# A decoder layer on one core: attention in two steps for a head pair, banks and small sums rearranged

## The reference, cut to what matters

```python
h = modulate(rms_norm(x, g_ffn1), sh1, sc1)
x = x + 0.5 * (1 + gt1) * swiglu(h, w1, w3, w2)
h = modulate(rms_norm(x, g_mix), sh2, sc2)
cq, ckv, kidx, widx, mq, mk, mv, ga, gb = split_cols(h @ w_in)
y_dsa  = dsa_attention(...) @ w_proj_dsa     # 8 heads, top-128 keys by an index score
y_moba = moba_attention(mq, mk, mv) @ w_proj_moba   # 8 heads, causal
y = sigmoid(ga) * y_dsa + sigmoid(gb) * y_moba
x = x + (1 + gt2) * (y @ w_out)
h = modulate(rms_norm(x, g_ffn2), sh3, sc3)
x = x + 0.5 * (1 + gt3) * swiglu(h, w1b, w3b, w2b)
out = rms_norm(x, g_final)
```

## Time and profile before

| | us |
|---|---|
| median of 3 runs | 1148.05 (1146.92 to 1148.19) |
| profiled execution, own time | 1148.91 |
| its span | 1147.0 |
| PE busy | 1121.8 |
| VectorE busy | 564.9 |
| ScalarE busy | 502.2 |
| mean granted PE clock | 0.997 |

### The profile page before, as it was taken

One profiled execution on the slowest core, in us unless ns is written; L12 is line 12 of the kernel. 1 busy time (PEld: TensorE's weight loads), 2 busy tenths in 40 slices (PEclk: granted clock), 3 DMA queues, 4 the chain that ended last, 5 costly groups with the idle time before them and its releaser, 6 DMA issues.

```text
span 1147.0 us, 14769 instructions
## 1 busy us (share of the span) xinstructions
PE 1121.8 (98%) x5421; PEld 902.0 (79%) x5421; DVE 564.9 (49%) x912; ACT 502.2 (44%) x874; POOL 182.1 (16%) x114
## 2 busy tenths in 40 slices
PE   6999999999999999999999999999999999999998
PEld 4678888888888868877776778877888888888887
DVE  3544454444344475489884537677333333332232
ACT  4565646555444443244555654444232332232233
POOL 0055454454333510000000000040000000000000
PEclk9999999999999999999999999999999999999999
DMA  9846655665555333222212123322332332243221
GB/s 307 282 147 191 224 170 179 196 211 174 175 174 174 91 90 104 55 56 74 55 38 74 52 60 92 92 74 74 110 110 73 101 118 73 91 134 101 78 74 74
DMA packets 159099, 138.25 MB, mean 121 GB/s; under 512 B 3551, under 2 KB 157522, under 8 KB 159058
## 3 DMA queue, kind: packets, MB, share of 16 engines
q1 hardware_dynamic: 130948, 109.38, 30.7%
q10 hardware_dynamic: 28110, 28.32, 7.6%
HBM read 135.59 MB, written 2.10 MB: 120 GB/s over the span
## 4 chain that ended last, share of the span: by engine, by line
PE 86%; DVE 7%; SPq 3%; ACT 2%; DMA 1%; issue 1%; POOL 0%; ACTq 0%; DVEq 0%; POOLq 0%
PE ps L373 26%; PE ps L375 26%; PE ps L374 26%; SPq L926 2%; PE ps L1150 2%; PE ps L1177 2%; PE ps L1161 2%; DVE w_lo L352 2%; DVE score L1534 1%; DMA raw<-in_w_ffn 1%; DVE max L1532 1%; SPq L932 1%; DVE tmp L444 1%; ACT w_hi L347 1%; PE ps L500 1%
## 5 line engine op out<-in xcount | busy, mean ns | idle before, releaser
L352 DVE TENSOR_TENSOR w_lo<-raw,w_hi 128x1024 fp32r<-128x1024 f32 (+1 forms) x164 | 239.2, 1459 | 375.9 <-ACT w_hi L347 375.9
L373 PE MATMUL ps<-h_hi,w_hi 128*128 128x512 f32 x1008 | 400.6, 397 | 7.9 <-DVE w_lo L352 4.7
L375 PE MATMUL ps<-h_hi,w_lo 128*128 128x512 f32 x1008 | 393.7, 391 | 0.0
L374 PE MATMUL ps<-h_lo,w_hi 128*128 128x512 f32 x1008 | 393.0, 390 | 0.0
L347 ACT ACTIVATE w_hi<-raw 128x1024 fp32r<-128x1024 f32 (+1 forms) x164 | 183.5, 1120 | 362.1 <-PE ps L375 361.7
L373 PEld LDWEIGHTS ps<-h_hi,w_hi 128*128 128x128 f32 x1008 | 189.7, 188 | 54.8 <-issue 9.7
L375 PEld LDWEIGHTS ps<-h_hi,w_lo 128*128 128x128 f32 x1008 | 189.5, 188 | 40.9
L374 PEld LDWEIGHTS ps<-h_lo,w_hi 128*128 128x128 f32 x1008 | 189.9, 188 | 37.6 <-issue 0.2
L373 PE MATMUL ps<-g_hi,w_hi 128*128 128x512 f32 x330 | 129.9, 394 | 0.1
L375 PE MATMUL ps<-g_hi,w_lo 128*128 128x512 f32 x330 | 128.6, 390 | 0.0
L374 PE MATMUL ps<-g_lo,w_hi 128*128 128x512 f32 x330 | 128.5, 389 | 0.0
(11 more groups left out here) (217 smaller groups left out, 1010.6 us busy)
## 6 DMA issues: line engine op xcount, KB each, us to landing
raw<-in_w_ffn SPq DMA_DIRECT2D x42, 1024.0 KB, 5.4
ada<-in_w_ada ACTq DMA_DIRECT2D x27, 1024.0 KB, 5.1
raw<-in_w_ffn SPq DMA_DIRECT2D x16, 1408.0 KB, 6.3
raw<-in_w_in SPq DMA_DIRECT2D x64, 256.0 KB, 3.2
ada<-in_w_ada SPq DMA_DIRECT2D x16, 512.0 KB, 8.8
raw<-in_w_out SPq DMA_DIRECT2D x16, 256.0 KB, 3.0
x_tok<-in_x SPq DMA_DIRECT2D x4, 512.0 KB, 5.4
raw<-in_w_ffn SPq DMA_DIRECT2D x8, 256.0 KB, 7.3
```

Of the source, the lines that this page charges most:

```text
L352: nc.vector.tensor_tensor(tiles_of(w_lo[j % SPL], nk), raw_of(f, j, nk), tiles_of(w_hi[j % SPL], nk).bitcast(F32), ALU.subtract).then_inc( ...
L373: nc.tensor.matmul(ps[:, bank, :], hi, rhs_hi, start=start, stop=False)
L374: nc.tensor.matmul(ps[:, bank, :], hi, rhs_lo, start=False, stop=False)
L375: return nc.tensor.matmul(ps[:, bank, :], lo, rhs_hi, start=False, stop=stop)
```

## The change

It does seven things.

- `pe_sums_and_shift` becomes `pe_token_sums` and `pe_factors_and_shift`. The sums are taken with tokens on the partitions, one column for each 128 tokens; ScalarE's square root and VectorE's reciprocal work on 4 columns; VectorE spreads them over a diagonal (`dve_diag`), and after two more tiles PE multiplies that by ones to get the factors in PSUM. `dve_scaled` reads them there, and a copy goes to `tmp` for the unscaling.
- The unscaled pair uses banks 6 and 7 (`B_Y`) and waits for the modulation sums and not for the last residual.
- `pe_second_pair` works four tiles of unit 3, four of unit 4, then the last four of unit 3, then of unit 4.
- The fifth unit's split is at the end of `dve_h` and `act_h`, ahead of the unscaling; in the second FFN the sixth follows in the unscaled pair's step. The first iteration's units in the second FFN and the fifth and sixth unit of the mixer no longer wait for banks 0 and 1.
- Attention has two steps for a head pair: chunks 0, 1 and 2 together, and chunk 3. So there are 16 steps. Scores of chunk 1 of both heads, and the last two transposed blocks of both heads, share bank 6; PE waits for its own first matmul there before the other head's. All values go to bank 7. Scores also wait for the copies of the step before last.
- Gate tiles come eight in the first two iterations and seven after that; selections two or three an iteration; the mask stands after step 7; the gate copy and `o_high` stand ahead of the exponentials.
- Three value tiles come after the first gate tiles, the fourth in the next iteration; ScalarE copies them.

```diff
+        def pe_token_sums(pe, n):
             pe.wait_ge(acc_done, 6 * n)
-            nc.tensor.matmul(ps[:, B_SUM, :], ones[:, :], tmp[:, 2, :], start=True, stop=False)
             pe.wait_ge(sq_done, KD * n)
-            nc.tensor.matmul(ps[:, B_SUM, :], ones[:, :], tmp[:, (KD - 1) % 2, :], start=False, stop=True).then_inc(sum_done, 1)
+            for t in range(QT):
+                nc.tensor.matmul(ps[:, B_SUM, t:t + 1], tmp[:, 2, t * P:(t + 1) * P], ones[:, 0:1], start=True, stop=False)
+                last = nc.tensor.matmul(ps[:, B_SUM, t:t + 1], tmp[:, (KD - 1) % 2, t * P:(t + 1) * P], ones[:, 0:1],
+                                        start=False, stop=True)
+            last.then_inc(sum_done, 1)
+        def pe_factors_and_shift(pe, n):
+            pe.wait_ge(diag_done, n + 1)
+            nc.tensor.matmul(ps[:, B_SUM, :], ones[:, :], tmp[:, 3, :], start=True, stop=True).then_inc(row_done, 1)
 ...
         def dve_h(dve, n, u):
-            dve.wait_ge(shift_psum, n)
-            nc.vector.tensor_copy(shift[:, :], ps[:, B_MOD, 0:2]).then_inc(shift_done, 1)
             dve.wait_ge(sqrt_done, n + 1)
-            nc.vector.reciprocal(tmp[:, 3, :], tmp[:, 3, :]).then_inc(rstd_done, 1)
+            dve_diag(dve, tmp[:, 3, :], rtok[:, :], diag_done, n + 1 + (2 if n == 2 else 0))
+            dve.wait_ge(row_done, n + 1)
 ...
             dve_low(dve, n, KD - 1)
+            dve.wait_ge(shift_psum, n)
+            nc.vector.tensor_copy(shift[:, :], ps[:, B_MOD, 0:2]).then_inc(shift_done, 1)
+            nc.vector.tensor_copy(tmp[:, 3, :], ps[:, B_SUM, :]).then_inc(factor_done, 1)
+            lo_u(dve, u + 4)
+            dve.wait_ge(factor_done, n)
 ...
         def act_h(act, n, u):
-            nc.scalar.activation(tmp[:, 3, :], ps[:, B_SUM, :], ACT.Sqrt, bias=eps[:, :]).then_inc(sqrt_done, 1)
+            nc.scalar.activation(rtok[:, :], ps[:, B_SUM, 0:QT], ACT.Sqrt, bias=eps[:, :], scale=1.0 / D_MODEL).then_inc(sqrt_done, 1)
 ...
+            hi_u(act, u + 4)
 ...
         def pe_second_pair(pe, n, u):
-            order = [(q, k) for q in range(2) for k in range(half)] + [(q, k) for k in range(half, KD) for q in range(2)]
+            order = [(q, k0 + k) for k0 in (0, half) for q in range(2) for k in range(half)]
 ...
-        CHUNKS = (((0, 0), (1, P)), ((2, 0),), ((3, 0),))
+        CHUNKS = (((0, 0), (1, P), (2, 3 * P)), ((3, 0),))
-        B_S, B_T, B_O = (0, 1), (2, 3), (6, 7)
+        B_S, B_T, B_X, B_O = (0, 1), (2, 3), 6, 7
+        PARTS = (((0, 1, B_X, 0, 4), (1, 1, B_X, 2 * P, 4), (0, 0, B_S[0], 0, 5), (0, 2, B_S[0], P, 5),
+                  (1, 0, B_S[1], 0, 6), (1, 2, B_S[1], P, 6)),
+                 ((0, 0, B_S[0], 0, 1), (1, 0, B_S[1], 0, 2)))
+        SCORE_ORDER = ((0, 4, 2, 1, 3, 5), (0, 1))
-            take = min(5, GATE_TILES - given)
+            take = min(8 if m < 2 else 7, GATE_TILES - given)
 ...
             def scores(m):
-                pe.wait_ge(m_done, 2 * m)
-                for n, (c, at_) in enumerate(cs):
-                    for e in range(2):
-                        o = 64 * e
-                        last = nc.tensor.matmul(ps[:, B_S[e], at_:at_ + (c + 1) * P], q[o:o + 64, hp, c * P:(c + 1) * P],
+                pe.wait_ge(m_done, parts_before(m))
+                if m >= 2:
+                    pe.wait_ge(pt_done, m - 1)
+                parts = list(parts_of(m))
+                for i in SCORE_ORDER[m % SPP]:
+                    e, n, c, at_, dst, _ = parts[i]
+                    o = 64 * e
+                    if m % SPP == 0 and i == 1:
+                        pe.wait_ge(s_psum, parts_before(m) + 1)
+                    nc.tensor.matmul(dst, q[o:o + 64, hp, c * P:(c + 1) * P], k[o:o + 64, hp, 0:(c + 1) * P],
+                                     start=True, stop=True).then_inc(s_psum, 1)
 ...
             for m in range(NST + 3):
                 for g in gates_ended(m - 1):
                     hi_u(act, U_GATE + g + 2)
+                    nc.scalar.activation(gate[g][:, :], ps[:, 4 + g % 2, :], ACT.Copy).then_inc(evac, 1)
+                if m > SPP and m % SPP == 1 and m < NST + 2:
+                    o_high(m // SPP - 1)
                 if m < NST:
                     exps(m)
```

More of the change, by code:

```diff
@@ L590, in pe_ffn @@
                 pe_second_pair(pe, 2, U_UP[f] + 2)
-            with pe.Fori(2 - f, KF // 2) as i:
+                for j in range(4):
+                    up(1, j)
+            with pe.Fori(2, KF // 2) as i:
                 for j in range(4):
@@ L686, in act_pair @@
                     .then_inc(silu_done, 1)
-            if not first and not unscaled:
+            if unscaled:
+                hi_u(act, U_UP[1] + 5)
+            elif f == 1 and isinstance(i, int) and i == 0:
+                pass
+            elif not first:
                 if f == 0:
@@ L730, in dve_pair @@
             else:
-                if not first:
+                if not first and not (f == 1 and isinstance(i, int) and i == 0):
                     for q in (2, 3):
@@ L877, in build_layer, with parts_of, parts_before, banks_before @@
         NST = len(steps)
-        def keys_of(m):
-            return sum((c + 1) * P for c, _ in steps[m][2])
-        B_S, B_T, B_O = (0, 1), (2, 3), (6, 7)
+        B_S, B_T, B_X, B_O = (0, 1), (2, 3), 6, 7
[3 more added lines that the diff above has]
+        SCORE_ORDER = ((0, 4, 2, 1, 3, 5), (0, 1))
+        def parts_of(m):
+            for e, n, bank, col, ready in PARTS[m % SPP]:
+                c, at_ = steps[m][2][n]
+                yield e, n, c, at_, ps[:, bank, col:col + (c + 1) * P], parts_before(m) + ready
+        def parts_before(m):
+            return sum(len(PARTS[i % SPP]) for i in range(m))
+        def banks_before(m):
+            return sum((3, 2)[i % SPP] for i in range(m))
+        VALUE_BANK = (B_O, B_T[0], B_T[1], B_O)
         OUT_BANK = (2, 3, 0, 1)
@@ L1155, in transposes @@
             def transposes(m):
+                blocks = sum(c + 1 for c, _ in steps[m][2])
                 for e in range(2):
                     pe.wait_ge(p_done, 2 * m + e + 1)
[L1158 to L1161, removed]
-                                                   ident[:, :])
+                    if m == 0:
+                        pe.wait_ge(vt_done, e + 2)
+                    else:
+                        pe.wait_ge(pt_done, m)
+                    for s in range(4):
+                        last = nc.tensor.transpose(ps[:, B_T[e], s * P:(s + 1) * P], prob[m % SPP][:, e, s * P:(s + 1) * P],
+                                                   ident[:, :])
+                    last.then_inc(pt_psum, 1)
@@ L1163, in transposes @@
+                if blocks > 4:
+                    for e in range(2):
+                        for s in range(4, blocks):
+                            o = (2 * e + s - 4) * P
+                            last = nc.tensor.transpose(ps[:, B_X, o:o + P], prob[m % SPP][:, e, s * P:(s + 1) * P], ident[:, :])
                     last.then_inc(pt_psum, 1)
@@ L1176, in values @@
                         for e in range(2):
-                            last = nc.tensor.matmul(ps[64 * e:64 * e + 64, B_O[pair % 2], c * P:(c + 1) * P],
+                            last = nc.tensor.matmul(ps[64 * e:64 * e + 64, B_O, c * P:(c + 1) * P],
                                                     v[:, s, hp * P + 64 * e:hp * P + 64 * e + 64],
@@ L1193, in _ @@
                     gate_tile(i)
+                if m == 0:
+                    for t in range(3):
+                        value_tile(t)
             for q in range(KD):
@@ L1454, in _ @@
             dve_unscale(dve, U_LAT, (cq[:, 0, :], cq[:, 1, :]))
-            for q in range(2, 4):
-                lo_u(dve, U_LAT + q + 2)
+            lo_u(dve, U_QKV + 1)
             lo_u(dve, U_QKV + 2)
```

151 lines of the change are left out of this document (73 added, 78 removed).

## The result

The changed kernel takes 1140.60 us in the median (1139.91 to 1142.24, 4 runs), the one before 1148.08 beside it: ratio 0.9927, interval 0.9908 to 0.9947. The forecast was 1139.9 in a range from 1136.0 to 1144.5. The profiled execution took 1140.5 us with a span of 1138.6; the forecast for that one was 1140.7 and 1138.8.

A forecast was written before the change was run, and what follows sets the result against it. TensorE bounds the kernel, busy 1121.8 of 1147.0 us. Gains of 2.3 (first transition), 2.9 (second) and 3.0 (attention with merge) sum to 8.2 us, giving 1139.9 us, range 1136.0 to 1144.5.

The forecast's parts named there:

- Small sums and factors: RMSNorm transitions: PE gets about 1.05 us more each, the 3.35 us reciprocal goes, the lead is mostly given back.
- Pair order and early split: Fifth unit's split ready before the second pair ends; gains 2.3 us at the first transition, 2.9 at the second.
- the chain of h_lo: First transition: from sums at 405.05 to the last h_lo at 424.0, so the pair ends at 427.55.
- the rival of a late split: Fifth split's 0.3 us margin is used up at both transitions, waits of 1.95 and 2.45 return: 1144.3 us; chance 0.14.
- Attention: First scores to merge: seams -2.8, dearer scores +1.7, waits -2.1, new wait +0.65; sum -2.5 us.
- three-chunk block: Attention's scores of chunks 0, 1 and 2 take 1.92 us, within bounds of 1.50 and 2.76.
- The wait at step 2: Attention: PE waits 0.65 us for ScalarE's copies, landing at 541.2 against 540.6 on PE, as VectorE starts late.
- the seams: Attention: 26 iterations with gate tiles become 18 at 0.344 us of seams each, 2.8 us less.
- The rival of heads in series: Attention: heads of unequal length don't overlap, three-chunk step 2.76 us, 6.7 more, 1146.6 us; chance 0.08.
- that of a hidden wait: Attention: score wait hidden behind other weight loads, three-chunk steps of 1.50 us, 3.4 less, 1136.5 us; chance 0.10.
- The rule of strict order in start and end: Attention's scores: matmuls strictly FIFO; each three-chunk step about 0.15 us more, time about 1.2 above forecast; chance 0.02.
- VectorE's load: Attention's first pairs: VectorE 90% full, about 17.5 us each; costs nothing, as results are wanted an iteration later.

The follow-up runs named there:

- large sums: Changed kernel with token sums, square root and reciprocal over 512 columns as before, no diagonal or factor matmul; 1140.51 us.
- the edits that take either half away: Changed kernel with the second pair's old tile order, 1145.24 us; changed kernel with fifth and sixth units' splits back behind the unscaling, 1144.75 us.
- new score order: Changed kernel with head 1's own bank first and its shared-bank matmul last in attention's three-chunk step; 1136.58 us.
- loaded kernel: Changed kernel with one unused VectorE sum over 1024 columns added in each of attention's steps 2 to 7; 1141.61 us.
- late fifth split: Changed kernel with the fifth and sixth units' splits back behind the unscaling, new pair order kept; 1144.75 us.
- attention alone: Kernel before with only the attention part of the change; sums, pair order, unscaled pair's banks and splits as before; 1145.38 us.
- no selections in step 0: Kernel with the new score order, with no selection in attention's step 0, so selections end a step later; 1135.92 us.
- the spread: Kernel with the new score order, the latents' 24 one-column records spread over four weight-unit tiles, index-key transposes ahead of them; 1135.85 us.
- combined kernel: Changed kernel with new score order, spread one-column records of the latents' norms and no selections in attention's step 0; 1134.57 us.

## Why the prediction came out right, step by step

**Small sums and factors.** Right in each size, and in the judgement that their lead is mostly given back: the first scaled product starts at 408.69, and the large sums cost only 0.26 and 0.24 us more. That giving back was read off the queue: ScalarE's split of unit 3 waits for PE, not for the factor.

**Pair order and early split.** Right in mechanism: no `w_lo` wait at either place, and the edits that take either half away bring it back. 0.3 too much at the first, 0.2 at the second. The step that was off is the chain of h_lo: 405.05 to 424.0 is 18.95 us from the sums, and it took 423.59 - 404.39 = 19.20. So the pair ended 0.25 later than I had it. The margin of the split, 0.3 in the forecast, was 0.15 at both places: the rival of a late split (chance 0.14) was that near.

**Attention.** -2.46 against -2.5, but partly by errors that cancel. The three-chunk block took 2.03 and not 1.92, 0.9 us more over eight. The term that was too small is head 1's stream behind its wait: the forecast let it go on at 0.85 and take 1.07, but its 256 columns start 0.75 us into the block and the block ends 1.28 later, which is 1.07 and the 0.22 of a block's start once more. The wait at step 2 was 0.17 and not 0.65, 0.5 less: the copies landed at 538.39, where I had 541.2 for a kernel 2.6 us later at this point (538.6), and PE wanted them at 538.37, 0.4 later than I had it. The waits for `mvT`, `gate` and `prob` went as said. What the seams gave wasn't measured by itself; by difference it is 2.46 + 1.7 + 0.9 + 0.2 - 2.1 = 3.1, where I had 2.8.

One check on the seams: a steady pair without its gate tiles and scores is 18.35 - 15 x 0.68 - 2.77 = 5.38 us before and 17.65 - 14 x 0.68 - 3.09 = 5.04 after, so an iteration less saves 0.34, the forecast's 0.344. It also says what the reader should know of the title's change: two steps save about 3.1 us of seams and cost 2.6 of dearer scores, so they gain about half a microsecond, and most of attention's 2.46 is waits that went. With the new score order a pair's scores take 1.50 + 1.06 = 2.56 us, less than before, and the two steps gain about 4.8, less the 1.0 of waits that come back. No run has the steps without the moved value tiles, gate copy and selections.

The rival of heads in series (2.76 a block) is excluded by 2.03; that of a hidden wait (1.50) is excluded for this order, and the new score order shows that it was the right figure for one in which the wait is hidden.

The Trainium skill says under PSUM — Partial Sum Buffer, PSUM bank collisions raise a hardware error, that two row tiles of TensorE must not write one bank at the same time. That is why both orders keep a wait between the heads; no run here left it out, so this case doesn't show what would happen. What it shows is the price: 0.53 us a block where the wait stands ahead of the longer rest, nothing that shows in the block where it stands ahead of the last matmul.

The rule of strict order in start and end that the Trainium skill gives (TensorE: Matmul & The Clock Gate, The mechanism), and which the prediction weighed, isn't borne out by the new kernels either. The changed kernel's block doesn't decide it: by the prediction's estimate for the rule it would take 0.15 us more than 1.92, and it took 0.11 more. The new score order does. There head 1's first 384-column record starts 0.33 us into the block (the one at 554.74), and head 0's 128 columns, issued ahead of it, only at 0.54. And neighbours of unequal length (256 and 128, 128 and 384, 384 and 256 columns) take 1.50 us together, which is 6 x 0.213 and 0.22, as two streams of their own would.

**VectorE's load.** It stood at 92% over the first four pairs, with one at 96% and one full, where I had 90% for each, and cost nothing beyond the 0.17 at step 2, because its results are wanted an iteration later. The loaded kernel shows how much the lead bears: 7.2 us more of work cost PE 1.64. With the new score order, where PE comes sooner, VectorE's lateness at the start did cost 1.0.

**Sum.** 7.8 us in the profiled executions by the changed steps against 8.2. The spans happened to differ by 8.4, as the head of this execution was 0.66 shorter; that the span came within 0.2 us of the forecast is luck to that extent. By the medians it is 7.5, and the forecast missed by 0.7 us, a third of what I had called measurable.

## What to carry to other kernels

Where two buffers are held until a pair of units ends, stagger the ends of the two and put the next preparation into the gap in the engine's queue: here neither edit alone gave more than 0.75 us where both gave 2.00 and 2.70, so test such edits in pairs. Where two streams must not be in one bank at once, put the shared bank's matmul last in the stream that waits, behind its own work. An engine at 96%, or full for one pair, was no bottleneck here, as its results had an iteration of lead; look for waits at the start of the loop, where the lead isn't built yet.

## What the runs showed of the hardware

PE's granted clock falls from its upper level (2.4 GHz) to the lower (1.2 GHz) for about 3.4 us right behind the block of 24 one-column records at the latents' norms, in the kernel before too, though PE shows no gap. PE's timeline of the changed kernel, and its windows by the granted clock (the third number from the end):

```profile
440.19 0.58 PE L1094 MATMUL ps<-ones,lat_sq 128*128 128x1 f32 x4
440.64 0.56 PE L1095 MATMUL ps<-ones,lat_sq 128*128 128x1 f32 x2
441.06 0.69 PE L1100 MATMUL ps<-ident,kiw 68*128 68x68 f32 x4
...
442.51 0.63 PE L375 MATMUL ps<-h_hi,w_lo 128*128 128x512 f32 x1
442.93 0.63 PE L373 MATMUL ps<-h_hi,w_hi 128*128 128x512 f32 x1
...
444.15 0.40 PE L373 MATMUL ps<-h_hi,w_hi 128*128 128x512 f32 x1
444.39 0.40 PE L374 MATMUL ps<-h_lo,w_hi 128*128 128x512 f32 x1
```
```profile
437.40:440.70 3.30, 3.30 (x28) 3.14 (x26) 1.08 (x1) 2.17 (x4) 0.00 (x0) 0.99 0.44 121
440.70:444.10 3.40, 3.40 (x13) 2.92 (x13) 2.38 (x13) 2.06 (x4) 0.00 (x0) 0.50 0.57 150
```

The matmuls of 512 columns are 0.43 us apart there, and 0.23 on either side. The stretch from the latents' norms to attention's first scores is 82.5 to 82.6 us in the executions with the fall and 80.98 in the two without (the new score order, and the late fifth split), so it costs 1.6. In two executions (attention alone, and no selections in step 0) it lasted 6.8 us and the stretch was 84.1 to 84.2. The execution of attention alone shows two more falls of about 3.4 us, at 430.3 and 795.5, each behind a wait for the fifth split, and each transition is 1.6 us longer for it; the profile of the kernel before has the same two waits and no fall behind them. With the records spread over four tiles both profiles, of the spread and of the combined kernel, show full clock there:

```profile
440.70:444.10 3.40, 3.40 (x22) 2.94 (x20) 3.33 (x14) 2.49 (x5) 0.00 (x0) 1.00 0.45 113
```

and their runs lie within 0.9 and 1.1 us, where those with the block and the same score order lie within 3.2 and 3.7. The mean granted clock on record for every run fits this: 0.998 or 0.999 in all nine runs with spread records, 0.996 to 0.999 in the ten with the block, and a fall of 3.4 us takes 0.0015 off the mean. That the block brings on the fall is likely by this; it isn't certain, as of the ten profiles with the block two show no fall, and only one execution of each kernel was profiled.
